# Eight-block attention kernel: token-wise sums in the differential output, and five edits between stages

## The reference, cut to what matters

```python
def rms_norm(x, g):
    xf = x.astype(jnp.float32)
    y = xf * lax.rsqrt(jnp.mean(xf * xf, axis=-1, keepdims=True) + EPS)
    return (y * g.astype(jnp.float32)).astype(x.dtype)

def diff_attend(q, k, v, lam):
    s = jnp.einsum('bqhmd,bkhmd->bhmqk', q * (DIFF_HD ** -0.5), k)
    p = jax.nn.softmax(s.astype(jnp.float32), axis=-1)
    a = (p[:, :, 0] - lam * p[:, :, 1]).astype(v.dtype)
    return jnp.einsum('bhqk,bkhd->bqhd', a, v)

def diff_post(o, subln, lam_init):
    b, n = o.shape[:2]
    return (rms_norm(o, subln) * (1.0 - lam_init)).reshape(b, n, DIFF_HEADS * DIFF_V)

# in hybrid_layer, for layer l:
h_lat = rms_norm(x, norm_g) * (1.0 + scale) + shift
h_ctx = rms_norm(ctx, norm_g) * (1.0 + scale_c) + shift_c
# mla_heads:
q  = (rms_norm(qc, q_norm) @ w_uq)      # rank 384
kv = (rms_norm(kvc, kv_norm) @ w_ukv)   # rank 256
# merge_branches:
terms.append(jax.nn.sigmoid(gr) * ((y * jax.nn.silu(zr)) @ w_branch[r]))
```

## Time and profile before

| | |
|---|---|
| median of 3 runs | 4311.13 us (4303.09 to 4312.06) |
| the profiled execution, its own time | 4305.82 us |
| its span | 4304.0 us |
| mean granted clock of TensorE | 0.951 of full |
| PE / DVE / ACT busy | 3832.1 / 2169.0 / 1391.3 us |
| DMA | 275.36 MB, mean 64 GB/s |

### The profile page before, as it was taken

The page is one execution under the profiler, slowest core; times in us unless marked ns, Lnnn a source line. Parts: engine busy times, 40 slices in busy tenths (PEclk is TensorE's granted clock), DMA queues, the critical chain, the costliest instruction groups (busy, mean ns, idle before and its releaser), DMA issues. The chain is left out here.

```text
span 4304.0 us, 56060 instructions
## 1 busy us (share of the span) xinstructions
PE 3832.1 (89%) x20877; PEld 2926.4 (68%) x20877; DVE 2169.0 (50%) x3457; ACT 1391.3 (32%) x2476; POOL 0.2 (0%) x4
## 2 busy tenths in 40 slices
PE   4988979998689999999798998977999999798998
PEld 2655758876457787777586666865667777576666
DVE  3555345543455525777524555243563677535544
ACT  2433233322233313444312443121332444314432
POOL 0000000000000000000000000000000000000000
PEclk8999999998899999999899999988999999899999
DMA  6443325531100121111121101211103111121122
GB/s 234 139 113 94 92 83 166 163 115 69 35 25 24 33 61 45 39 34 34 35 64 33 27 25 31 68 39 38 33 28 84 52 45 39 54 69 30 35 59 73
DMA packets 504242, 275.36 MB, mean 64 GB/s; under 512 B 56665, under 2 KB 489781, under 8 KB 504094
## 3 DMA queue, kind: packets, MB, share of 16 engines
q1 hardware_dynamic: 483186, 252.08, 20.7%
q10 hardware_dynamic: 20908, 21.26, 1.6%
HBM read 271.08 MB, written 10.32 MB: 65 GB/s over the span
## 5 line engine op out<-in xcount | busy, mean ns | idle before, releaser
L559 PE MATMUL ps<-h_high,w_high 128*128 128x512 f32 (+1 forms) x3512 | 1309.5, 373 | 173.7 <-DVEq L2341 129.8
L559 PE MATMUL ps<-h_low,w_high 128*128 128x512 f32 (+1 forms) x3512 | 1279.0, 364 | 0.0
L559 PE MATMUL ps<-h_high,w_low 128*128 128x512 f32 (+1 forms) x3512 | 1275.5, 363 | 0.0
L559 PEld LDWEIGHTS ps<-h_high,w_high 128*128 128x128 f32 x3512 | 672.1, 191 | 324.6 <-DVEq L2341 137.2
L555 DVE TENSOR_TENSOR w_low<-w_raw,w_high 128x1024 fp32r<-128x1024 f32 x378 | 453.8, 1201 | 642.5 <-ACT w_high L545 618.7
L559 PEld LDWEIGHTS ps<-h_high,w_low 128*128 128x128 f32 x3512 | 671.2, 191 | 105.8
L559 PEld LDWEIGHTS ps<-h_low,w_high 128*128 128x128 f32 x3512 | 672.3, 191 | 96.6 <-issue 2.2
L545 ACT ACTIVATE w_high<-w_raw 128x1024 fp32r<-128x1024 f32 x378 | 392.2, 1039 | 784.8 <-PE ps L559 606.6
L781 ACT ACTIVATE probs<-ps,neg_max 128x768 f32<-128x768 f32 (+2 forms) x368 | 289.5, 789 | 641.5 <-DVE neg_max L806 441.2
L559 PE MATMUL ps<-probsT,v 128*128 128x512 f32 (+4 forms) x736 | 286.9, 559 | 10.3 <-DVE probsT L999 8.8
L559 PE MATMUL ps<-k_high,q_high 64*128 64x256 f32 (+4 forms) x784 | 185.9, 397 | 116.1 <-ACT probs L781 57.9
(11 more groups left out here) (200 smaller groups left out, 4030.4 us busy)
## 6 DMA issues: line engine op xcount, KB each, us to landing
w_raw<-in_w_in SPq DMA_DIRECT2D x444, 256.0 KB, 3.1
y_and_merged<-in_w_mod SPq DMA_DIRECT2D x96, 256.0 KB, 3.1
w_raw<-in_w_branch SPq DMA_DIRECT2D x96, 256.0 KB, 3.0
w_raw<-in_w_up SPq DMA_DIRECT2D x88, 256.0 KB, 4.2
y_and_merged<-in_w_ada SPq DMA_DIRECT2D x64, 256.0 KB, 3.3
w_raw<-in_w_out SPq DMA_DIRECT2D x48, 256.0 KB, 3.0
w_raw<-in_w_down SPq DMA_DIRECT2D x44, 256.0 KB, 2.8
y_and_merged<-in_w_ada SPq DMA_DIRECT2D x4, 2048.0 KB, 21.0
```

Source lines behind the costliest of these rows:

```text
L559: return nc.tensor.matmul(*a, **kw)
```

## The change

Six edits in one diff:

1. **diff output.** The sum of squares takes the squares as weights and two columns of ones as the moving side: tokens come out on partitions, one column for each block of 128 tokens. Root and reciprocal then work on 128 x 6 (layer 1: 128 x 4) numbers. PE spreads them back over the features, with `ORS` broadcast as weights and the identity as the moving side (`pe_ospread`), three steps into the next head's z split. DVE multiplies z by gain and spread, then `y` is one product.
2. **context rows.** Both `ctxload` stages are gone. The DMAs are issued at the start of `down` and of the last merge; PE's transposes stand at the start of `norm gfinal` and of `out`, DVE's copies there too (in `out` behind the eight `m_low`).
3. **latent norms.** The stages qn and kvn are gone. Their squares, sums, root, reciprocal and scaling are in `pre`: PE's sums of the q latent behind split 3, those of the kv latent at the end; DVE's part of the q latent behind the copy of split 4, that of the kv latent at the end. PE waits for `lat_n` in mla, before the q and the kv product.
4. **first split after a norm.** For h1, h2 and layer, PE doesn't wait at the fence; the first split waits for each `h_low` block in turn (`low_row`). PE doesn't wait at the fence of `pre` either.
5. **earlier `w_low`.** In h2 and layer, DVE makes it before it waits for the root.
6. **swapre.** Two splits of 128 key columns in place of four with doubled columns; ACT and DVE copy each half to both halves of the partitions. Four splits in place of six.

```diff
-            st += [Stage("ctxload")]
...
-        st += [Stage("norm", what="qn", nk=3, size=384, ctx=cq, l=l), Stage("norm", what="kvn", nk=2, size=256, ctx=True, l=l)]
...
-                for lo, n, b in groups:
-                    v.reciprocal(EB[:, 0, lo:lo + n], EB[:, 0, lo:lo + n])
-                v.drain()
-                for lo, n, b in groups:
-                    v.scalar_tensor_tensor(out=EB[:, 0, lo:lo + n], in0=bank(b, n), scalar=GS[:, s["l"]:s["l"] + 1],
-                                           in1=EB[:, 0, lo:lo + n], op0=ALU.mult, op1=ALU.mult)
+                nt = 6 if cq else 4
+                v.reciprocal(ORS[:, 0:nt], ORS[:, 0:nt]).then_inc(S["o_ri"], 1)
+
+                dve.wait_ge(S["o_sp"], cnt(s, "o_sp", t, per, po + 1))
+                for lo, n, b in [(0, LAT, bank(4))] + ([(LAT, CTX, bank(7, CTX, 256))] if cq else []):
+                    v.scalar_tensor_tensor(out=Z[:, lo:lo + n], in0=Z[:, lo:lo + n], scalar=GS[:, s["l"]:s["l"] + 1], in1=b,
+                                           op0=ALU.mult, op1=ALU.mult)
...
-            for lo, n, b in groups:
-                last = mm(bank(b - 1, n), ones[:, :], EB[:, 0, lo:lo + n], start=True, stop=True)
+            for tt in range(6 if s["cq"] else 4):
+                last = mm(bank(6, 2, 2 * tt), EB[:, 0, 128 * tt:128 * tt + 128], ones[:, 0:2], start=True, stop=True)
             last.then_inc(S["o_ss"], 1)
+
+        def pe_ospread(pe, s, t, u):
+
+            pe.wait_ge(S["o_ri"], cnt(s, "o_ri", t, s["unroll"], u + 1))
+            for tt in range(6 if s["cq"] else 4):
+                dst = bank(4, 128, 128 * tt) if tt < 4 else bank(7, 128, 256 + 128 * (tt - 4))
+                last = mm(dst, ORS[:, tt:tt + 1].to_broadcast([128, 128]), ident[:, :], start=True, stop=True, skip_group_check=True)
+            last.then_inc(S["o_sp"], 1)
...
+        def act_latent(act, s, g):
+
+            act.wait_ge(S["lat_ss"], s.base["lat_ss"] + g + 1)
+            for lo, n, ps in latent_parts(s, g, 0):
+                last = act.activation(LRS[:, g, lo:lo + n], ps, ACT.Sqrt, scale=1.0 / (128 * len(LROWS[g])), bias=EPSB[:, :])
+            last.then_inc(S["lat_rs"], 1)
...
+                    pe_split(pe, s, 0, 0, j, m, tgroups(2 * (j % 2), s["cq"] or j >= 3, m), ready="low_row" if j == 0 else None, since=8)
+                    if j == 3:
+                        pe_latent(pe, s, 0)
...
+                for j, c in enumerate((C_SK, C_SK + 128, C_SV, C_SV + 128)):
+                    load_split(sp, s, 0, 0, j, cols(win2[l], c))
...
-            eng.drain().then_inc(s_fence, 1)
-            eng.wait_ge(s_fence, 3 * (s.index + 1))
+            eng.drain().then_inc(s_fence[me], 1)
+            if me == "pe" and (s.kind == "pre" or s.kind == "norm" and s["what"] in ("h1", "h2", "layer")):
+                return
+            for other in s_fence:
+                if other != me:
+                    eng.wait_ge(s_fence[other], s.index + 1)
```

More of the change, by code:

```diff
@@ L125, in plan @@
     st += [Stage("norm", what="h2", nk=8, size=D, ctx=False), Stage("up"), Stage("down")]
-    st += [Stage("norm", what="gfinal", nk=8, size=D, ctx=False)]
+    st += [Stage("norm", what="gfinal", nk=8, size=D, ctx=False, rows=True)]
     for l in range(2):
@@ L559, in mm, with split_steps @@
             return nc.tensor.matmul(*a, **kw)
-        def split_steps(pe, s, t, per, off, m, groups, high=HR, low=HL, k0=0, nk=NK, ready=None):
+        def split_steps(pe, s, t, per, off, m, groups, high=HR, low=HL, k0=0, nk=NK, ready=None, since=0):
             k = raw_slot(s, t, per, off)
@@ L1022, in qk_steps @@
             if name == "mla":
+                if not ahead:
+                    pe.wait_ge(S["lat_n"], s.base["lat_n"] - 1)
                 k = pe_wait_plain(pe, s, t, 2, u)
@@ L1042, in qk_steps @@
             else:
-                yield from split_steps(pe, s, t, s["nh"], 0, 128, tgroups(0, cq))
+                opens = s["name"] == "dil" and not ahead
+                yield from split_steps(pe, s, t, s["nh"], 0, 128, tgroups(0, cq), ready="low_row" if opens else None, since=8)
                 if ahead and name == "diff":
@@ L1129, in pe_proj_z @@
             elif name == "diff":
-                pe_split(pe, s, t, 4, 3, 128, tgroups(2, s["cq"]))
+                steps = split_steps(pe, s, t, 4, 3, 128, tgroups(2, s["cq"]))
+                if beside is not None:
+                    few(steps, 3)
+                    beside()
+                for _ in steps:
+                    pass
         def act_q_out(act, s, t, u):
@@ L1765, in norm_source, with pe_rows, dve_rows, act_rows @@
                     (CT[:, kc, :], LAT, CTX, AC[:, 3 + 2 * l, kc:kc + 1], MOD[:, b, 1:2])]
+        def pe_rows(pe, s):
+            pe.wait_ge(S["ctx_in"], s.base["ctx_in"] + 32)
+            for j in range(4):
+                for e in range(2):
+                    for a in range(2):
+                        kc = 2 * j + e
+                        last = nc.tensor.transpose(bank(4 + j, 128, 256 * e + 128 * a), SQ_ROWS[:, a, 128 * kc:128 * kc + 128], ident[:, :])
+                last.then_inc(S["x_t"], 1)
+        def dve_rows(dve, s):
+            for j in range(4):
+                dve.wait_ge(S["x_t"], s.base["x_t"] + 8 + j + 1)
+                nc.vector.tensor_copy(CT[:, 2 * j:2 * j + 2, :], bank(4 + j).rearrange("p (e t) -> p e t", e=2))
+        def act_rows(act):
+            c = w["ctx_2"][0].rearrange("(a p) d -> p a d", p=128)
+            for a in range(2):
+                act.dma_start(SQ_ROWS[:, a, :], c[:, a, :]).then_inc(S["ctx_in"], 16)
         def pe_norm(pe, s):
+            if s["rows"]:
+                pe_rows(pe, s)
             for kc in range(s["nk"]):
@@ L1801, in dve_norm @@
             v = nc.vector
+            split = s["what"] in ("h1", "h2", "layer")
+            if s["rows"]:
+                dve_rows(dve, s)
+            if s["what"] in ("h2", "layer"):
+                dve_low(dve, Stage("first", h_end=None).at(s.base), 0, 0, 0)
             dve.wait_ge(S["rstd"], s.base["rstd"] + 1)
@@ L1806, in dve_norm @@
             v.drain()
-            split = s["what"] in ("h1", "h2", "layer")
-            if split:
+            if s["what"] == "h1":
                 dve_low(dve, Stage("first", h_end=None).at(s.base), 0, 0, 0)
@@ L2364, in _ @@
                 pe_stage(pe, s)
-                fence(pe, s)
+                fence(pe, "pe", s)
         @block.scalar
@@ L2370, in _ @@
                 act_stage(act, s)
[L2371 removed]
+                fence(act, "act", s)
         @block.vector
```

159 lines of the change are left out of this document (94 added, 65 removed).

## The result

The changed kernel takes **4211.34 us** (median of 4 runs, 4210.58 to 4212.22) against 4309.58 for the kernel before, run beside it: a ratio of 0.9774 (95% interval 0.9757 to 0.9791). That is 98 us won where the prediction had 111. The time lies inside the range (4178 to 4220), 11 us above the forecast. The profiled execution took 4210.58 us, its span is 4208.8 (4304.0 before), the mean granted clock 0.958.

What follows compares the result with a forecast made beforehand. PE was busy most of the span, so gains come where it stands still or does less. Terms 6.5 - 15.4 - 45.4 - 23.8 - 33.3 = -111.4 us take 4311.1 to 4200 us; range 4178 to 4220.

Steps and rivals of the forecast that it cites:

- 1. The diff output: Diff heads: sums and spread lengthen inner heads by 1.45 us (layer 0) and 0.4 (layer 1), tails shorten; +6.5 us.
- costs nothing: Rival for the diff heads: parallel spread passes, full reciprocal slack and a favourable clock make the edit free; 4191 us, chance 0.12.
- 2. Context rows: Both context loads go (-8.9, -9.1); `gfinal` transposes cost 1.8, `down` 0.8, `out` nothing; -15.4 us.
- 3. Latent norms: From the last split of `pre` to the kv product's end, 24.1 and 21.3 us are won; -45.4, plus or minus 5.
- T: The end of the last split in `pre`, forecast to move later by 3.9 us in layer 0 and 2.6 in layer 1.
- The rival of a longer latent chain: In `pre`, ACT or DVE come late to the root, moving later work some 4 us per layer; 4209 us, chance 0.1.
- 4, 5. First splits and earlier `w_low`: After norms, second splits start sooner in up, `pre` and after h1, `w_low` gives 3.7; -23.8 us, plus or minus 5.
- 7.5 to 3.6: 3.9: After h1, the first split's stretch falls from 7.5 to 3.6 us behind the fence, winning 3.9.
- late transfers: Sign that the prediction is wrong: transfers come late now that PE asks for them sooner; no size given.
- a PEclk at 0.5: Sign that the prediction is wrong: PEclk in the stretches after norms stays at 0.5.
- 6. swapre: In `swapre`, two splits of 8.33 us fewer in each layer, all PE's own time; -33.3 us.
- half clock: Rival: PE's bursts leave later splits, mla starts, kv products and transposes slow, some 16 us; 4216 us, chance 0.15.

Runs made afterwards that it cites:

- experiment 1: The changed kernel with the new diff output undone in all 16 heads, the other edits kept: 4200.24 us, ratio 0.9743.
- experiment 2: The kernel before the change with the new diff output alone added: 4323.48 us, ratio 1.0032.
- experiment 9: The changed kernel with every matmul of the diff output's spread issued twice: 4224.52 us, ratio 0.9806.
- experiment 5: The changed kernel with ACT's 3.8 MB write for na's biases issued behind the bias load of dil's second head: 4216.52 us, ratio 0.9788.
- experiment 6: The changed kernel with the 3.8 MB write moved behind dil's second bias load and PE waiting at h1's fence again: 4221.50 us, ratio 0.9799.
- experiment 7: The changed kernel with PE waiting again at the fences of h1, h2 and both layers' norms: 4225.69 us, ratio 0.9804.

## Why the prediction was right, and where it was off

The mechanism was right nearly everywhere; the term for the first split after h1 failed, and that for the diff output in layer 0 was too small. Edits 2, 3, 5 and 6 were not undone by themselves; what they gave is read from the stages in which they fall. By the prediction's own steps:

**1. The diff output, +6.5 forecast; 11 and 12 us measured in the medians by undoing it and by making it alone, 9.6 and 9.8 in the diff stages of those traces, 9.2 from before to after.** The price of an inner head in layer 0 was 1.45 us; measured 1.38 from head to head (57.4 against 56.05), 1.26 of it the spread and the rest the sums, which take 1.36 us to the next split where the old ones took 1.21 (the prediction had them "as before"). The row of equal weight columns was the right one to take, and it was right that the weights set the pace: a pass takes 0.11 us with two columns and with 64, and 0.105 with 128. The issue floor of about 25 ns in the section "Back-to-back issue gap" of "TensorE: Matmul & The Clock Gate" in the Trainium skill, taken by itself, would have put the twelve passes of the sums at 0.3 us, an estimate; the trace after has 1.36. In layer 1 a head grew by 0.26 us (0.4 forecast), as the wait on `y`, 4.1 us over seven heads before, is gone. Where the wait on `y` went in layer 0 was right too: 2.3 us of it are gone in the stage, and the waits for the exponentials grew from 16.7 to 19.1. The tail of the last head is 2.7 us shorter in layer 0 where the forecast had 4.0, since its spread runs at the low clock (2.93 us for 1.50), and 2.4 in layer 1 as forecast. What no term had are the low-clock spells in two inner heads of layer 0, 1.55 us each: 3.1 us. Seven times 1.4, plus 3.1, less 2.7 is 10.2 of the stage's 10.3. The rival "costs nothing" is refuted by experiments 1, 2 and 9.

**2. Context rows, -15.4 forecast, -18.2 measured** (-8.3 and -9.8). The stretch of `out` took 13.1 us for 13.2, so the transposes and copies are as hidden as forecast. `down` is 1.0 longer (0.8 forecast). The term of 1.8 for the transposes in `gfinal` was too high: with them the stage is 20.3 us long, 20.7 before.

**3. Latent norms, -45.4 forecast, -46.0 measured.** T moved by 3.7 us (3.9) and 2.2 (2.6). From there to the end of the kv product it took 19.2 us (20.0 forecast) and 18.4 (17.6): T + 22.9 and T + 20.6 where 23.9 and 20.2 stood, won 25.1 and 20.9. The chain is as told: DVE's q latent scaling delays the last copy in layer 0, and the kv product waits for the scaling. One wait was missing: in layer 0 the kv reciprocal starts at T + 9.4 instead of 8.4, as it waits for ACT's root behind the sums on PE:

```profile
1159.92 4.95 DVE L1906 RECIPROCAL y_and_merged<-y_and_merged 128x768 f32<-128x768 f32 x1 [1.64 <-ACT y_and_merged L1898]
```

The clock behaved in neither layer as the middle value of 4.2 had it: the product took 2.79 us at full, 5.38 at the low clock. These two misses, -1.4 and +1.2, cancel, so that the sum came out within 1 us is in part luck. The rival of a longer latent chain, 4 us in each layer, didn't come about.

**4, 5. First splits and earlier `w_low`, -23.8 forecast, about -16 measured.** Up gave 6.5 (6.8). In the layers the pause before the second split shrank as forecast (up to its start 6.5 and 5.7 us won, forecast 6.7 and 6.3), but in layer 1 3.0 us of it were given back in the splits behind it, which begin at the low clock; in layer 0 they run at 1.00 and give back 0.2. After h1 nothing was won, and this is the step that failed: "7.5 to 3.6: 3.9". The second split did start at 81.84, 3.7 after the fence; but the third block's weights land behind ACT's write of 3.8 MB (experiments 5 and 6), so PE waited there instead. The prediction named late transfers as what would make it wrong, and didn't look at dil's third block. It named a PEclk at 0.5 behind the norms too, and that sign came as well, in the first splits of `pre` (0.55 and 0.50 in the stretches above). The early `w_low`, 3.7 of the forecast, was not measured by itself; experiment 7 has none of it in h2 and up.

**6. swapre, -33.3 forecast, -33.0 measured** (18.0 and 15.0, the difference between the layers being one low-clock spell).

**The rest, +8.8 in stages with the same code.** The largest are na (+2.9), the first model's out (+2.5) and layer 1's last merge (+1.7). In the profiles of the experiments, with that code unchanged, na takes 161.9 to 164.4 us, that out 47.8 to 49.1 (47.8 in experiment 2, where all ahead of it is the kernel before) and that merge 92.0 to 93.7. So a part of the difference between the two profiles isn't the change's: it comes and goes from one execution to the next. How much of it comes back in the median can't be read from one profile each. The two profiles are 95 us apart where the sum had 111. Of the 16 us between, some 8 are in the first splits, 2.6 in the diff stages and 8.8 in the unchanged code; the context rows, 2.8 better than forecast, and the latent norms, 0.6, are set against them. The medians are 98 apart; the prediction set out from 4311.1 for the kernel before, which took 4309.6 beside the changed one. The rival "half clock" was right in three places (the splits behind the bursts in layer 1, its kv product, the spread of the tail in layer 0) and too large in size: the splits behind the bursts gave back 3 us, in `pre` of layer 1. The spells in two diff heads, 3.1 us, were in no rival.

## What to carry to other kernels

Before you take work off an engine for a form that costs TensorE passes, look for the wait that it would end: here the reciprocal fell from 4.96 to 0.19 us (3.35 to 0.19 in layer 1) in 14 heads and only made TensorE, the bound, longer, by 1.4 us in each head of layer 0 and by 0.3 in layer 1, while the same form paid in the last head of each layer and in one latent norm, where nothing lay beside the reciprocal. Price the passes at the clock of the place: 0.105 us each in dense work, 0.2 at the low clock, where the same form was a loss of 20 us in the norms. And when a stage may start sooner, follow its third weight block as well as its first, with all other transfers in flight at that time.

## What the runs showed of the hardware

- A float32 matmul pass with 128 weight columns takes 0.105 to 0.11 us at full clock with 2, 64 or 128 columns on the moving side, and 0.20 to 0.23 at the low clock. So the moving columns don't set it.
- Low-clock spells of 3.4 us came in the midst of heads with a busy TensorE (granted clock 0.50 from 1714.6 to 1718.0), in layer 0 at the same two gaps in five of six profiles of kernels with the new form in all heads, two columns and a single spread (at the first of the two alone in the sixth), and at these gaps in no profile with the old form. Each costs 1.55 us. What sets them off stays open: the run with 64 columns had none in its profile, and the one with a doubled spread, with two columns, had none either.
- A write of 3.8 MB issued once held back the loads of 256 KB beside it: issued at 78.7 us, it let a load issued at 82.22 land only at 103.06; with the write moved the same load, issued at 83.76, landed at 87.28. Issued at 148.1 us instead, the write let other loads issued at 151.8 to 155.8 land at 165.9 to 173.8, and PE waited 12.7 us.
